# A hybrid encoder layer on one core: q projected as channels, and the last convolution's streams' part moved in among the mixers' work

## The reference, cut to what matters

```
xn = rmsnorm(x, norm_mix_w)
proj = xn @ w_in                      # [2048 prompt tokens + 8 streams x 16 tokens, 1024] x [1024, N_IN]
fq, fk, fv, ff, gqkv, ga, gb, gz = split(proj)   # 512, 512, 512, 8, 1536, 4, 4, 512 columns
# forgetting attention, 8 heads x 64
logits = (q . k) * 64**-0.5 + cq - ck, causal;  o_fox = softmax(logits) @ v
# gated DeltaNet, 4 heads x 128
qkv = silu(causal_conv4(concat(conv_state, gqkv)));  new_conv = last 3 rows
o_gdn = chunked delta rule(l2norm(gq), l2norm(gk), gv, g, beta)
h = x + concat(o_fox, rmsnorm(o_gdn) * silu(gz)) @ w_o
... = h + w_down(silu(conv3(gate)) * conv3(val)), final rmsnorm
```

## Time and profile before

| | |
|---|---|
| median of 3 runs | 3906.06 us (3905.84 to 3911.61) |
| the profiled execution | 3911.97 us |
| its span, first to last instruction | 3910.1 us |
| TensorE busy in the span | 3743.0 us, 96% |
| VectorE, ScalarE, GpSimd busy | 42%, 30%, 8% |
| mean granted TensorE clock | 0.983 |

### The profile page before, as it was taken

How to read it: one execution, slowest core, us unless ns; L and a number is a source line. 1 busy time by engine, 2 the same in 40 slices (tenths; PEclk the granted TensorE clock), 3 DMA queues, 4 the chain that set the end, 5 groups by cost and what they waited for, 6 DMA issues and landing times. The chain is left out here.

```text
span 3910.1 us, 54760 instructions
## 1 busy us (share of the span) xinstructions
PE 3743.0 (96%) x20924; PEld 3237.5 (83%) x20924; DVE 1627.5 (42%) x3502; ACT 1172.4 (30%) x2328; POOL 328.4 (8%) x404
## 2 busy tenths in 40 slices
PE   8999999899999999999998999999999999799998
PEld 8999999777777777676676889999999999688886
DVE  4000477545544454444434444444444444432222
ACT  5112222233333333332213333333333333221111
POOL 3000000211111111211200000000000000000000
PEclk9999999899999999999989999999999999899999
DMA  4221232310222212024433431111111111342222
GB/s 153 70 69 63 61 90 70 79 40 24 60 45 45 51 26 47 18 62 162 145 118 108 130 93 45 47 44 44 44 49 52 45 46 34 116 145 81 81 81 68
DMA packets 359100, 278.86 MB, mean 71 GB/s; under 512 B 129890, under 2 KB 324818, under 8 KB 358871
## 3 DMA queue, kind: packets, MB, share of 16 engines
q1 hardware_dynamic: 349503, 258.03, 22.4%
q0 software_dynamic: 4896, 17.83, 1.3%
q10 hardware_dynamic: 4524, 0.55, 0.1%
HBM read 190.70 MB, written 85.65 MB: 71 GB/s over the span
## 5 line engine op out<-in xcount | busy, mean ns | idle before, releaser
L2455 PE MATMUL bank<-ffn_hn_hi,ffn_w_parts 128*128 128x436 f32 (+1 forms) x3520 | 985.5, 361 | 2.1 <-ACTq L2524 2.1
L2455 PEld LDWEIGHTS bank<-ffn_hn_hi,ffn_w_parts 128*128 128x128 f32 x3520 | 662.2, 188 | 39.0 <-issue 2.5
L2455 PE MATMUL bank<-ffn_hn_lo,ffn_w_parts 128*128 128x436 f32 (+1 forms) x1760 | 634.8, 361 | 0.0
L2455 PEld LDWEIGHTS bank<-ffn_hn_lo,ffn_w_parts 128*128 128x128 f32 x1760 | 331.3, 188 | 19.5
L2550 ACT COPY ffn_raw<-bank 128x436 f32<-128x436 f32 (+1 forms) x220 | 110.3, 501 | 706.0 <-PE bank L2455 653.2
L394 PE MATMUL bank<-in_wh,in_xh 128*128 128x256 f32 (+1 forms) x1088 | 308.0, 283 | 0.0
L394 PE MATMUL bank<-in_wh,in_xl 128*128 128x256 f32 (+1 forms) x1088 | 307.5, 283 | 0.0
L394 PE MATMUL bank<-in_wl,in_xh 128*128 128x256 f32 (+1 forms) x1088 | 305.9, 281 | 0.0
L1528 PE MATMUL bank<-heads_p_pT,heads_p_v 128*65 128x512 f32 (+3 forms) x640 | 287.5, 531 | 10.7 <-issue 10.1
L2652 DVE TENSOR_SCALAR ffn_hist<-ffn_raw 128x2 f32 (+2 forms) x264 | 45.0, 171 | 551.9 <-ACT ffn_acc L2554 549.2
L407 PE MATMUL bank<-in_xh,in_wh 128*128 128x436 f32 (+1 forms) x960 | 267.4, 360 | 1.0 <-DVE in_wh L617 1.0
(11 more groups left out here) (407 smaller groups left out, 6535.6 us busy)
## 6 DMA issues: line engine op xcount, KB each, us to landing
ffn_w<-in_w_up_dram SPq DMA_DIRECT2D x44, 512.0 KB, 5.0
down_g_raw<-scratch_g SPq DMA_DIRECT2D x110, 192.0 KB, 2.4
scratch_g<-ffn_acc SPq DMA_DIRECT2D x88, 218.0 KB, 2.0
heads_s_k<-in_cache_fox_k_dram SPq DMA_DIRECT2D x8, 2048.0 KB, 13.4
heads_s_v<-in_cache_fox_v_dram SPq DMA_DIRECT2D x8, 2048.0 KB, 8.4
heads_d_qkvT<-scratch_gch SPq DMA_DIRECT2D x17, 768.0 KB, 5.6
down_y<-in_w_down_dram SPq DMA_DIRECT2D x22, 512.0 KB, 3.2
scratch_gch<-in_work SPq DMA_DIRECT2D x48, 218.0 KB, 1.9
```

Of the source, the lines that this page charges most:

```text
L2455: mm = pe.matmul(bank[:, pair(n) + e, 0:width], w_parts[a][:, part, e, k, :], x[:, k, cols], start=(k == 0 and m == 0), stop=(k == KD - 1 ...
```

## The change

q is no longer projected as two row pieces but as four blocks of 128 channels ahead of the twelve of `gqkv`. ScalarE copies such a chunk straight to `acc`, SP stores it to a scratch tensor `qch` (channels by tokens), and there is no convolution. The prompt's attention loads q of a head already turned, 64 channels by 2048 tokens, twice (upper and lower 64 partitions); TensorE's turning of q and its PSUM uses go, and ScalarE and VectorE read q from SBUF (`q_scalar`, `q_vector`). The streams' q is loaded turned as well.

The load of the first chunk of channels is issued one store earlier. Of the last chunk's convolution, only the prompt's part stays ahead of the mixers' work; the streams' part, its SiLU and its store get later due times. Some due times of the mixers' start move.

```
-    pieces = [(0, halves), (halves, FW), (FW, FW + halves), (FW + halves, 2 * FW),
+    pieces = [(FW, FW + halves), (FW + halves, 2 * FW),
...
-    weights = pieces + [(off_g + ch * P, off_g + (ch + 1) * P) for ch in range(NCH)]
+    NQ = FW // P
+    weights = pieces + [(ch * P, (ch + 1) * P) for ch in range(NQ)] + [(off_g + ch * P, off_g + (ch + 1) * P) for ch in range(NCH)]
...
+            if i < Q:
+                sp.wait_ge(chan_raw, i + 1)
+                rows_of = io["qch"][i // NK * P:(i // NK + 1) * P, :]
+            else:
+                sp.wait_ge(silu_done, i - Q + 1)
+                rows_of = io["gch"][(i - Q) // NK * P:((i - Q) // NK + 1) * P, :]
+            sp.dma_start(rows_of[:, col:col + wide], acc[i % 2][:, 0:wide]).then_inc(chan_stored[i % 2], 16)
...
+                if n == 2 and ch == NQ + NCH - 1:
+                    sp.wait_ge(chan_stored[ch * NK % 2], 16 * (ch * NK // 2 + 1))
+                    first_tokens(sp)
-            if ch == 2:
+            if ch == NQ:
...
-        a = (NCH - 1) * NK
-        sp.wait_ge(chan_stored[a % 2], 16 * (a // 2 + 1))
-        first_tokens(sp)
...
     def last_sync(sp):
-        yield -17.5
+        yield 10.0
...
     def last_tensor(pe):
-        yield 0.7
+        yield 11.0
...
+            if i < Q:
+                if i >= 2:
+                    act.wait_ge(chan_stored[i % 2], 16 * (i // 2))
+                wide = chunks[n][1]
+                nc.scalar.copy(acc[i % 2][:, 0:wide], bank[:, 4 + i % 2, 0:wide]).then_inc(chan_raw, 1)
+                return
...
     def last_scalar(act):
-        yield -5.0
+        yield 8.5
...
         yield -9.0
-        conv(dve, i)
-        yield -3.0
+        conv(dve, i, 0)
+        yield 6.9
+        conv(dve, i, 1)
+        yield 11.9
         tail_out(dve, 2)
...
+        for ch in range(NQ):
+            split_lo(NR + ch + 1)
...
-        uses = [(0.0, ("c", 0)), (9.0, ("c", 1))]
-        uses += [(1.0 + 1.5 * n, (("k", "q")[n // 4], 0, n % 4)) for n in range(8)]
+        uses = [(0.0, ("c", 0)), (4.9, ("c", 1))]
+        uses += [(1.0 + 1.5 * n, ("k", 0, n)) for n in range(4)]
+        self.q_at = {(0, n): 7.4 + 1.2 * n for n in range(4)}
...
     def load_q(self, sp, h):
         for e in range(2):
+            sp.dma_start(self.q_raw[e * self.FD:(e + 1) * self.FD, :],
+                         self.io["qch"][h * self.FD:(h + 1) * self.FD, 0:self.c["SEQ"]]).then_inc(self.s["q_loaded"], 16)
...
+    def q_scalar(self, act):
+        s, nc, FD = self.s, self.nc, self.FD
+        for (h, n), at in self.q_at.items():
+            cols = slice(n * BANK, (n + 1) * BANK)
+            yield at + 1.4
+            if n == 0:
+                act.wait_ge(s["q_loaded"], 32 * h + 32)
+                if h >= 2:
+                    act.wait_ge(s["key_mm"], self.first_key[(h - 1) * self.NG])
+            nc.scalar.mul(self.q_both[:, h % 2, cols], self.q_raw[:, cols], float(FD) ** -0.5)
+            nc.scalar.mul(self.q_hi[0:FD, h % 2, cols], self.q_raw[0:FD, cols], float(FD) ** -0.5) \
+                .then_inc(s["hi_ready"], 1)
+
+    def q_vector(self, dve):
...
+            yield at + 2.6
+            dve.wait_ge(s["hi_ready"], 8 * h + 4 + n + 1)
+            nc.vector.scalar_tensor_tensor(rows, self.q_raw[FD:P, cols], float(FD) ** -0.5, rows.bitcast(F32),
+                                           ALU.mult, ALU.subtract).then_inc(s["q_ready"], 1)
...
     # Sample.tensor, scalar, vector: the suffix sums
-        yield 23.0
+        yield 28.0
```

More of the change, by code:

```diff
@@ L427, in tensor @@
         mm.then_inc(small_turned, 1)
-        for ch in range(NCH):
+        for ch in range(NQ + NCH):
             pe.wait_ge(w_lo, NR + ch + 2)
@@ L431, in tensor @@
                 channel_products(ch, n)
-                if ch == NCH - 1 and n in (0, 2):
+                if ch == NQ + NCH - 1 and n in (0, 2):
                     after(pe, tail_ready, n // 2)
@@ L1330, in set_times @@
                 for n in range(4):
-                    uses.append((starts[G] + (starts[G + 1] - starts[G]) * (0.1 + 0.17 * n),
-                                 (("k", "q")[g - 1], h + 1, n)))
+                    part = starts[G] + (starts[G + 1] - starts[G]) * (0.1 + 0.17 * n)
+                    if g == 1:
+                        uses.append((part, ("k", h + 1, n)))
+                    else:
+                        self.q_at[h + 1, n] = part
         self.uses = sorted(uses)
@@ L1851, in tensor @@
         pe.wait_ge(s["new_loaded"], 48)
-        for n, src in enumerate((self.q_tok, self.k_tok)):
-            for p in range(NP):
-                mm = pe.transpose(self.bank[:, self.logit[n], p * P:(p + 1) * P], src[:, p * P:(p + 1) * P], ident)
-            mm.then_inc(s["new_turned"], 1)
+        for p in range(NP):
+            mm = pe.transpose(self.bank[:, self.logit[1], p * P:(p + 1) * P], self.k_tok[:, p * P:(p + 1) * P], ident)
+        mm.then_inc(s["new_turned"], 1)
         yield self.begin + 7.8
```

128 lines of the change are left out of this document (60 added, 68 removed).

## The result

| | before | changed |
|---|---|---|
| median of 4 runs | 3907.65 us | 3881.48 us (3877.54 to 3886.97) |
| profiled execution, span | 3910.1 us | 3880.8 us |
| ratio | | 0.9932, 95% interval 0.992 to 0.9945 |
| ratio, measured a second time | | 0.9936, 0.9922 to 0.9949 |

Faster by 26 us; 3880 was forecast. The spans of the profiled executions differ by 29.3 us. Cut at the same instructions, that difference falls apart as follows. The cuts are the first tile of the second row piece, the end of the projection's last matmul, the delta rule's first product of keys (line 913 before, 932 now) and the load of its fifteenth chunk (at 1730.48 and 1702.44).

What follows compares the result with a forecast made beforehand. The prediction took TensorE, busy 937.5 of 1000 us, to bound the kernel. Projection 1.8, start 9.2, body 14.9 and streams' q 0.4 sum to 26.3 us off the median of 3906.06, close to 3880; range 3866 to 3893.

Steps and rivals of the forecast that it cites:

- Projection, 1.8 us: Projection: two q row pieces removed (96.4 us), four channel blocks added (94.7 us); gain 1.8 us, bounds 0 and 3.
- come a head ahead: zero: Body: the two loads of turned q have fewer, longer runs and come a head ahead; cost zero.
- Start, 9.2 us: Mixers' start, up to the delta rule's first products: 4.7 + 1.3 + 2.6 + 3.6 - 1.3 - 1.7; bounds 4 and 13.
- Load: Start: first chunk's load issued one store sooner, TensorE's wait shrinking from 6.96 to 2.3 us; gain 4.7, bounds 2 and 7.
- Waits and slow turnings of q: Start: TensorE's waits for q pieces, 2.6 us, and the first head's four slow-clock q turnings, 3.6 us, both go.
- The move of the streams' part: Start: wait for `heads_d_S` gone, 1.3 us; against it a table load, 1.3, and VectorE work before first keys, 1.7.
- The table load, 1.3 us: Start: one more function table load on ScalarE ahead of the last chunk's SiLU, 1.28 us, no drain charged behind it.
- Body, 14.9 us: Body: 12.3 of TensorE work and 4.1 of waits gone, 1.5 charged for held q pieces; bounds 8 and 22.
- The matmuls, 12.3: Body: 28 uses of q turning leave TensorE at 0.44 us each, 12.3 us.
- The waits and held pieces: Body: two thirds of 6.1 us of output turnings' waits go, 4.1; VectorE's q pieces held by GpSimd cost 1.5.
- rival 1: Body: half its gain, 7 of 14.9 us, turns into waits such as those on row maxima; 3887 us, chance 0.20.
- Rival 4: Body: GpSimd holds each of VectorE's 28 q pieces up to 2.08 us, TensorE waiting; 58 us, total 3937, chance 0.02.

Runs made afterwards that it cites:

- both repairs: Changed kernel with the mixers' first loads one group per channel block and the first head's q pieces 3 due-time units later; ratio 0.992, median 3878.84 us.
- the streams' part ahead: Changed kernel with the last convolution's streams' part, its SiLU, store and last rows' turning back at old due times, ahead of the mixers' work; ratio 0.9944.

## Why the prediction was right, and where not

The total and the sign came out: 26.3 us forecast, 26 in the medians. The start and the body, where nearly all of it was expected, gave it, both inside their bounds. That the total fits this closely is luck: the projection came out 2.9 us under its forecast, the start and the body 1.4 and 2.2 over theirs, and the starts of one and the same work differ by 2.3 us by the clock.

- *Projection, 1.8 us: wrong, -1.1.* The pace of both ways was right to 0.05 us (96.45 for 96.4 removed, 23.67 a block). The step that failed is that the new loads of q "come a head ahead: zero", with the SP queue passed by at "a store per chunk": the loads of the start stand in one row ahead of channel stores, and the row cost 4.2 us where it had cost 1.3: 1.3 us more as a wait on weights (2.5 for 1.2), and 1.6 since the clock fell behind the longer wait. The kernel before showed that stall already, as a wait of 1.0 us on weights, and the prediction did not look at it.
- *Start, 9.2 us: 10.6, with its terms wrong.* The grant rose over the stretch from 0.66 to 0.82; with the grant of 0.67 the same instructions gave 8.3. Load: 3.6 for 4.7, the rest going to the convolution, which then stood in the way. Waits and slow turnings of q: 6.2 forecast, 0.6 when taken away alone, 1.9 to 4.2 behind the move. The move of the streams' part was costed at 1.3 - 1.3 - 1.7 = -1.7; it gave 2.8 alone and 4.1 to 6.4 with q gone. The step took only the wait for the state for VectorE's debt; in fact VectorE releases most of TensorE's waits in the start once the load is early, and its order of work is what counts. The 1.7 us at the new place cost nothing, since they fell into VectorE's wait for the fourth piece of k (the run that moved them away again gained 0.24).
- *The table load, 1.3 us.* Hidden when q's pieces stand behind the copies of the turned keys; in the changed kernel it and those pieces make the wait of 1.5 us on kb turned.
- *Body, 14.9 us: 17.1*, or 18.4 at the same grant. The matmuls, 12.3, measured about 10.5 by the experiment that puts them back. The waits and held pieces, 4.1 - 1.5 = 2.6, were too low: idle time fell by 4.1 us, and some 3 us more of busy time went with the uses of the bank, a term that the sum did not have. The waits on q went, and those on row maxima fell rather than grew, so rival 1 did not come.
- *Rival 4, slower.* Held pieces came to 1.8 us of VectorE's time (1.5 forecast). Its price of one us of kernel for each us held was too high: of 40.4 us more work, 12.1 reached TensorE as idle time and the body grew by 20.4, the clock included. At half a us for each, even 28 pieces held for 2.08 us each would cost 29 us, an estimate, and leave the kernel about where it was before.

## What to carry to other kernels

When one edit makes data arrive sooner, its worth ends where the next engine is late: ask at once what that engine has in front of it, since the edit that clears it is then worth more (here 0.6 and 2.8 us apart, 4.7 to 7.0 together). A row of loads on a queue that also stores what engines wait for has a price even if nobody waits for the loads: look at how long each issue takes, and spread them. Where steps of 1 to 3 us are in question, cut the traces at the same instructions and put the granted clock beside each time, since it alone moved the start by 2.3 us and the price of 112 matmuls from 8.0 to about 10.5; the runs of this kernel, some 10 us apart, can't tell such steps.

## What the runs showed of the chip

- **A MEMSET of GpSimd holds some instructions of VectorE.** A COPY of 24 columns took 3.53 us, beside a MEMSET of two partitions, and 0.18 when that was moved. It ended with the MEMSET. The Trainium skill, "SBUF — State Buffer", section "Who interferes with whom", says that VectorE's copies and `tensor_scalar` can enter a mode that takes the port pair shared with GpSimd, exclusively; these rows agree. VectorE's q piece at 731.22 of the changed kernel ran beside the same MEMSET and took its usual 0.69 us. The MEMSET writes 2 x 4096 elements in 3.51 us, one of 32 x 2048 takes 1.80: few partitions don't shorten the hold.
- **The clock at a start is not the kernel's alone.** With the same instructions and waits up to there, the first turnings of k behind the projection ran at 2.4 GHz in one run and at 1.2 in another, worth 2.3 us at kn. In the body, the same 5492 or 5493 matmuls were busy for 907.8 us with a grant of 1.00 and for 915.6 with 0.99 (both repairs, and the streams' part ahead), with idle times of 59.0 and 58.7. A start that is 1 to 2 us shorter in work can come out longer; only the rows with their durations tell the two apart.
- **A tiny load can hold a queue.** 4 KB took 7.02 us to issue behind 2 MB of loads, and 0.43 us apart from them.
